# Summing the retrieved v rows in 64x64 quarters of the PE array, in a one-core encoder layer

## Chip, core and metric

The kernel runs on one core of one Trainium2 chip. The metric is the device time of one execution in microseconds (us). Before the change it is 2211.79 us, the median of three runs (2210.6 to 2211.9).

## The reference

One encoder layer for 512 tokens of width 1024 in float32: a gated mixer of a state-space layer and latent attention, a cross-attention over 256 memory tokens, and a retrieval of single-neuron experts; then a final norm. The change lies in the retrieval. Per token and head (8 heads), 16 experts are picked out of 16,384 by two lists of 128 keys; each has a row u and a row v of 1024 floats.

```python
s1, i1 = lax.top_k(s[:, :, 0], PEER_TOPK)
s2, i2 = lax.top_k(s[:, :, 1], PEER_TOPK)
cand_s = (s1[..., :, None] + s2[..., None, :]).reshape(T, PEER_HEADS, PEER_TOPK * PEER_TOPK)
cand_i = (i1[..., :, None] * PEER_N_KEYS + i2[..., None, :]).reshape(...)
top_s, pos = lax.top_k(cand_s, PEER_TOPK)
idx = jnp.take_along_axis(cand_i, pos, axis=-1)
gate = jax.nn.softmax(top_s, axis=-1)
u = jnp.take(u_emb, idx, axis=0)
act = jax.nn.gelu(jnp.einsum('thkd,td->thk', u, xc).astype(jnp.float32))
vv = jnp.take(v_emb, idx, axis=0)
return jnp.einsum('thk,thkd->td', (gate * act).astype(vv.dtype), vv)
```

## The kernel before

The kernel is written engine by engine, each with its own instruction list and explicit semaphores. The mixers and the cross-attention fill roughly the first 800 us; the retrieval fills the rest.

The retrieval works on groups: group g = 4h + t is head h (0 to 7) and token tile t (0 to 3, 128 tokens on the 128 partitions). A group has 16 slots, one expert per token and slot. For each slot POOL issues one indirect DMA that gathers 128 rows of 4 KB, partition p getting the row of token p, from `peer_u` into a ring of 8 places (`Ub`) and from `peer_v` into one of 16 places (`Vb`).

Who does what in period g:

- POOL (`head`, L1873) issues u of slot s of group g+1 and v of slot s of group g in turn. It waits for `dots` before it reuses a place of `Ub` (L1865) and for `v_summed` before it reuses one of `Vb` (L1870). All gathers are recorded under L1860.
- DVE (`head`, L1384): in the third tile of a head it copies the next head's scores (L1332); it picks the 16 best for group g+2 (`topk`, L1336 to L1356); it adds the finished sum of group g-1 to the residual H (`take_sum`, L1376); it forms the 16 dot products of group g+1 as the u rows land (L1367); then the 16 weights of group g+1 (`weights`, L1371) and the gates of group g+2 (L1358). Each small instruction is waited for before the next.
- ACT (`head`, L885) copies queries, takes the exponentials of the gates of g+2, and turns each of the 16 weights of group g into a diagonal matrix of 128x128 (L882; a ring of 8, `DRING`), then the gelu of g+1 (L875).
- PE (`head`, L1735) forms the next head's queries (L1710) and scores (L1720) ahead of the first two tiles, and then the weighted sum as matmuls: diagonal times v rows, 2 halves of 512 columns for each slot, accumulated over the 16 slots in two of the banks 0 to 3 (L1731). Even and odd tiles use different pairs of banks, so PE waits only for the sum of group g-2.
- SP loads the next head's 1 MB of query weights once PE has used the last ones, and at the end stores the output.

After the last group DVE takes its sum and normalises the rows (L1401 to L1410).

Of the kernel before, what the change touches and what calls it, by code (L numbers as in the profile page):

```python
# [29 lines left out]
U32 = mybir.dt.uint32  # L30
ALU = mybir.AluOpType
# [3 lines left out]
P = 128  # L35
# [154 lines left out]
def encoder_layer(nc, x, mem, positions, g_mix, w_in, b_gate, ssm_lam_re, ssm_lam_im, ssm_log_dt,  # L190
# [4 lines left out]
    with ctx:  # L195
# [3 lines left out]
        def sem(name):  # L199
            return ctx.enter_context(nc.semaphore(name))  # L200
# [25 lines left out]
        def reg(lo, *shape, base=R, parts=P):  # L226
            n = int(np.prod(shape))
            v = base[0:parts, lo:lo + n]
            names = "abcd"[:len(shape)]
            if len(shape) > 1:  # L230
                v = v.rearrange(f"p ({' '.join(names)}) -> p {' '.join(names)}",
                                **dict(zip(names, shape)))
            return v
# [62 lines left out]
        qhs = [reg(0, T), reg(512, T)]  # L296
        SC = reg(1024, NT, 2, NK)
        Vb = [reg(3072 + D * i, D) for i in range(VRING)]
        diag = [reg(19456 + P * i, P) for i in range(DRING)]
        gprow = reg(23040, D)  # L300
        gfrow = reg(24064, D)
        prod = reg(25088, D)
# [55 lines left out]
            sem(n) for n in ("qw_in", "q_filled", "q_copied", "s_filled", "s_copied")]  # L358

        idx_ready, gates_neg, gates_exp = [sem(n) for n in ("idx_ready", "gates_neg", "gates_exp")]  # L360
        dots, gelu_done, w_ready, diag_done, v_summed = [
            sem(n) for n in ("dots", "gelu_done", "w_ready", "diag_done", "v_summed")]
        acc_taken, final_done = sem("acc_taken"), sem("final_done")
# [222 lines left out]
        def _(act):  # L586
# [274 lines left out]
            def queries_out(h, s, first=False):  # L861

                act.wait_ge(q_filled, h * 2 + (s + 1))
                if not first:
                    act.wait_ge(s_filled, h * 2 + (s - 1))
                cols = slice(P if first else 0, T)
                act.activation(qhs[s][:, cols], ps[4 + s][:, cols], ACT.Copy).then_inc(q_copied, 1)

            def gate_exponentials(g):
                act.wait_ge(gates_neg, g + 1)  # L870
                act.activation(ex, cv, ACT.Exp, bias=nmx, accum_out=esum).then_inc(gates_exp, 1)
# [5 lines left out]
            def diagonals(g, t, first=False, slots=range(TOPK)):  # L877
                act.wait_ge(w_ready, g + 1)
                for s in slots:
                    if not first or s >= DRING:  # L880
                        act.wait_ge(v_summed, g * TOPK + (s - DRING + 1))
                    act.activation(diag[s % DRING], ident, ACT.Copy,  # L882
                                   scale=wgt[t % 2][:, s:s + 1]).then_inc(diag_done, 1)

            def head(h, first=False, last=False):  # L885
# [17 lines left out]
            def final_root(t):  # L903
                act.wait_ge(var_done, len(PARTS) + t + 1)
                act.activation(stat[:, 72 + t:73 + t], stat[:, 68 + t:69 + t], ACT.Sqrt).then_inc(std_done, 1)

            queries_out(0, 0, True)
            queries_out(0, 1, True)
            gate_exponentials(0)
            gate_exponentials(1)  # L910
            gelu_of(0)
# [9 lines left out]
        def _(dve):  # L921
# [391 lines left out]
            def lstep(ins):  # L1313

                count[0] += 1
                ins.then_inc(c_loop, 1)
                dve.wait_ge(c_loop, count[0])
# [18 lines left out]
            def topk(t):  # L1336

                for s in range(2):
                    top16(SC[:, t, s, :], sc1, tv[:, s, :], ti[:, s, :])
                lstep(dve.tensor_copy(tif, ti))  # L1340
                lstep(dve.tensor_tensor(cand.rearrange("p (a b) -> p a b", a=TOPK),
                                        tv[:, 0, :].unsqueeze(2).to_broadcast([P, TOPK, TOPK]),
                                        tv[:, 1, :].unsqueeze(1).to_broadcast([P, TOPK, TOPK]), ALU.add))
                top16(cand, cand1, cv, cpos)
                lstep(dve.tensor_scalar(nmx, cv[:, 0:1], -1.0, None, ALU.mult))
                dve.sem_inc(gates_neg, 1)
                lstep(dve.tensor_scalar(cpp[:, 0:16], cpos, 4, None, ALU.logical_shift_right))
                lstep(dve.tensor_scalar(cpp[:, 16:32], cpos, 15, None, ALU.bitwise_and))
                lstep(dve.tensor_copy(cpf, cpp))
                lstep(dve.tensor_tensor(eq, iota16.unsqueeze(1).to_broadcast([P, 2 * TOPK, TOPK]),  # L1350
                                        cpf.unsqueeze(2).to_broadcast([P, 2 * TOPK, TOPK]), ALU.is_equal))
                e4 = eq.rearrange("p (s k) a -> p s k a", s=2)
                lstep(dve.tensor_tensor(e4, e4, tif.unsqueeze(2).to_broadcast([P, 2, TOPK, TOPK]), ALU.mult))
                lstep(dve.tensor_reduce(isel, eq, AX.X, ALU.add))
                lstep(dve.scalar_tensor_tensor(idx[t], isel[:, 0:16], float(NK), isel[:, 16:32], ALU.mult, ALU.add))
                dve.sem_inc(idx_ready, 1)  # L1356

            def gates_of(g, t):  # L1358
# [11 lines left out]

            def weights(g, t):  # L1371
                dve.wait_ge(gelu_done, g + 1)
                lstep(dve.tensor_tensor(wgt[t % 2], gel, gate[t % 2], ALU.mult))
                dve.sem_inc(w_ready, 1)

            def take_sum(g, t):  # L1376

                dve.wait_ge(v_summed, (g + 1) * TOPK)
                for n in range(2):
                    h = H[:, t, 512 * n:512 * n + 512]  # L1380
                    lstep(dve.tensor_tensor(h, ps[2 * (t % 2) + n][:, :], h, ALU.add))
                dve.sem_inc(acc_taken, 1)

            def head(h, first=False, last=False):  # L1384
# [56 lines left out]
        def _(pe):  # L1441
# [279 lines left out]
                ins.then_inc(s_filled, 1)  # L1721


            def group(g, t, taken=True):
                if taken:
                    pe.wait_ge(acc_taken, g - 1)
                for s in range(TOPK):
                    pe.wait_ge(ld_v[s], (g + 1) * 16)
                    pe.wait_ge(diag_done, g * TOPK + (s + 1))
                    for n in range(2):  # L1730
                        last = pe.matmul(ps[2 * (t % 2) + n][:, :], diag[s % DRING], Vb[s][:, 512 * n:512 * n + 512],  # L1731
                                         start=(s == 0), stop=(s == TOPK - 1))
                    last.then_inc(v_summed, 1)

            def head(h, first=False, last=False):  # L1735
                for t in range(NT):
                    if t < 2 and not last:
                        queries(h + 1, t)
                        scores(h + 1, t)
                    group(h * NT + t, t, taken=not first or t >= 2)  # L1740

            for b in range(8):
                pe.wait_ge(drained[b], uses[b])
# [11 lines left out]
        def _(pool):  # L1755
# [103 lines left out]
            def gather(dst, table, ix, s, signal):  # L1859
                pool.indirect_dma_start(out=dst, out_offset=None, in_=table,  # L1860
                                        in_offset=bass.IndirectOffsetOnAxis(ap=ix[:, s:s + 1], axis=0)).then_inc(signal, 16)
# [6 lines left out]
            def v_row(g, t, s, first=False):  # L1868
                if not first:
                    pool.wait_ge(v_summed, g * TOPK + (s - (VRING - 1)))  # L1870
                gather(Vb[s], peer_v, idx[t], s, ld_v[s])

            def head(h, first=False, last=False):  # L1873
                for t in range(NT):
# [49 lines left out]
```

## Time and profile before

| | |
|---|---|
| median of three runs | 2211.79 us |
| the profiled execution | 2210.13 us, of which the span of its instructions 2208.3 us |
| busy in the span | PE 1804.8 us (82%), DVE 1450.7 (66%), POOL 1168.7 (53%), ACT 557.3 (25%) |
| L1731, matmul of diagonals and v rows | 2048 records, 973.8 us busy |
| L1860, gathers | 1024, 537 MB of the 603 MB that DMA moves |
| L882, diagonals | 512, 180.5 us busy, 394 ns each |
| chain that ended last | PE 37%, POOL 25%, DVE 16%, issue 11%, DMA 8%, ACT 3% |

How to read it: busy times say how much an engine worked, not that it set the pace. A timeline row has the start, the duration, the engine, the line, the instruction with its operands, the count, and in brackets the idle time before it with what ended it; "issue" is idle time in which nothing visible was awaited. One matmul of float32 shows as two records. "Landing" is the end of a DMA, seen here as the start of the instruction that waited for it.

### The profile page before, as it was taken

The numbers are of one execution on the slowest core, as the hardware profiler recorded it, in microseconds if no ns is written. First come the engines' busy times: TensorE is split into PE (matmuls) and PEld (weight loads), VectorE is DVE, ScalarE is ACT, GpSimd is POOL, SyncE is SP. The second block draws the span as 40 slices with busy tenths as digits, with TensorE's granted clock in tenths as the row PEclk, the third lists the DMA queues.
The fourth block names the chain that finished last, engine by engine and source line by source line (L and its number), as shares of the span: only waits on it lengthen the run. The fifth ranks groups of instructions, "written<-read, shape, count | busy, mean of one in ns | idle before, by whom it ended". The sixth has DMA issues, their size and how long they took to land.

```text
span 2208.3 us, 19211 instructions
## 1 busy us (share of the span) xinstructions
PE 1804.8 (82%) x5927; PEld 979.4 (44%) x5927; DVE 1450.7 (66%) x2986; ACT 557.3 (25%) x1159; POOL 1168.7 (53%) x1175
## 2 busy tenths in 40 slices
PE   6787798999998973969868878977877877887687
PEld 6455534787996761423323323323323322333233
DVE  5497675434444447777677677767767776776763
ACT  2323444222433121222112212212211221221211
POOL 6990000000001016777777777777777777777774
PEclk9889699999999995989989999999999999999899
DMA  4311401334342028999999999999999999999997
GB/s 117 61 16 20 105 1 34 86 100 140 95 133 68 20 82 346 395 393 408 401 397 408 406 393 410 403 392 408 376 398 401 406 390 403 410 400 398 409 399 295
DMA packets 239391, 603.06 MB, mean 273 GB/s; under 512 B 38533, under 2 KB 105274, under 8 KB 239290
## 3 DMA queue, kind: packets, MB, share of 16 engines
q0 software_dynamic: 147840, 537.99, 62.0%
q1 hardware_dynamic: 91450, 63.85, 10.5%
q8 instruction: 49, 0.80, 0.2%
q14 instruction: 52, 0.43, 0.1%
HBM read 597.56 MB, written 2.10 MB: 272 GB/s over the span
## 4 chain that ended last, share of the span: by engine, by line
PE 37%; POOL 25%; DVE 16%; issue 11%; DMA 8%; ACT 3%; SPq 0%; DVEq 0%; ACTq 0%; POOLq 0%
PE bank L1458 20%; PE bank L1731 15%; POOL R L1860 11%; POOL WS L1860 6%; POOL slabs L1860 5%; DMA WS<-in_peer_u,R 4%; DMA R<-in_peer_v,R 3%; DVE R L931 3%; PE bank L1710 2%; DVE R L1367 1%; PE bank L1447 1%; POOL R L1764 1%; POOL WS L1764 1%; DVE R L1199 1%; DVE stat L1192 1%
## 5 line engine op out<-in xcount | busy, mean ns | idle before, releaser
L1731 PE MATMUL bank<-R 128*128 128x512 f32 x2048 | 973.8, 624 | 243.1 <-ACT R L882 143.2
L1731 PEld LDWEIGHTS bank<-R 128*128 128x128 f32 x2048 | 387.8, 198 | 820.3 <-issue 570.6
L1860 POOL DMA_INDIRECT R<-in_peer_v,R x512 | 502.0, 980 | 156.0 <-issue 139.5
L1367 DVE CUSTOM_DVE_ANT_0 R<-WS,XN 128x1024 f32<-128x1024 f32 x256 | 313.6, 1225 | 176.4 <-DMA WS<-in_peer_u,R 171.8
L1367 DVE CUSTOM_DVE_ANT_0 R<-slabs,XN 128x1024 f32<-128x1024 f32 x256 | 313.7, 1226 | 125.7 <-DMA slabs<-in_peer_u,R 115.0
L1860 POOL DMA_INDIRECT slabs<-in_peer_u,R x256 | 259.4, 1013 | 209.0 <-DVEq L1356 96.2
L1860 POOL DMA_INDIRECT WS<-in_peer_u,R x256 | 262.1, 1024 | 78.0 <-issue 78.0
L1856 POOL TENSOR_TENSOR FTr<-slabs,FTr 128x2048 fp32r<-128x2048 f32 x1 | 4.5, 4494 | 536.3 <-ACT FTr L624 536.3
L882 ACT ACTIVATE R<-cst,R 128x128 f32<-128x128 f32 x512 | 180.5, 394 | 345.4 <-PE bank L1731 343.6
L1458 PE MATMUL bank<-R 128*128 128x64 f32 (+5 forms) x596 | 190.7, 463 | 45.9 <-ACT R L680 19.8
L1458 PEld LDWEIGHTS bank<-R 128*128 128x128 f32 (+3 forms) x596 | 89.8, 183 | 118.9 <-issue 75.5
L875 ACT ACTIVATE R<-R 128x16 f32<-128x16 f32 x32 | 6.9, 216 | 479.1 <-DVE R L1367 479.1
L964 DVE TENSOR_TENSOR WSr<-slabs,WSr 128x1024 fp32r<-128x1024 f32 (+2 forms) x47 | 60.7, 1292 | 99.8 <-ACT WSr L624 99.8
L1710 PE MATMUL bank<-FT,slabs 128*128 128x512 f32 (+1 forms) x256 | 112.0, 592 | 14.2 <-DMA slabs<-in_w_peer_q 11.6
L931 DVE TENSOR_TENSOR R<-R 128x512 f32<-128x512 f32 (+4 forms) x95 | 74.1, 780 | 32.6 <-POOLq L1844 26.5
L1458 PE MATMUL bank<-Rr,WSr 128*128 128x512 f32 (+1 forms) x448 | 95.4, 366 | 0.0
L1458 PEld LDWEIGHTS bank<-Rr,WSr 128*128 128x128 f32 x448 | 77.7, 189 | 13.7
L1710 PEld LDWEIGHTS bank<-FT,slabs 128*128 128x128 f32 x256 | 49.6, 194 | 73.5 <-issue 57.7
L1447 PE MATMUL bank<-cst,R 128*128 128x128 f32 (+2 forms) x300 | 48.0, 297 | 25.8 <-DVE R L1199 21.9
L624 ACT ACTIVATE WSr<-slabs 128x1024 fp32r<-128x1024 f32 (+2 forms) x48 | 53.9, 1125 | 59.2 <-PE bank L1458 59.2
L1458 PE MATMUL bank<-XNr,WSr 128*128 128x512 f32 x256 | 61.8, 393 | 1.9 <-DVE WSr L964 1.9
L1458 PE MATMUL bank<-FTr,WSr 128*128 128x512 f32 x256 | 63.2, 389 | 0.1
(210 smaller groups left out, 1903.4 us busy)
## 6 DMA issues: line engine op xcount, KB each, us to landing
slabs<-in_w_in SPq DMA_DIRECT2D x17, 512.0 KB, 5.3
slabs<-in_w_mem_kv SPq DMA_DIRECT2D x8, 1024.0 KB, 5.6
slabs<-in_w_peer_q SPq DMA_DIRECT2D x8, 1024.0 KB, 16.3
R<-in_peer_v,R POOLq DMA_INDIRECT x512, 6.6
slabs<-in_w_in SPq DMA_DIRECT2D x4, 1024.0 KB, 13.1
slabs<-in_w_ssm_glu SPq DMA_DIRECT2D x16, 256.0 KB, 3.2
slabs<-in_w_out SPq DMA_DIRECT2D x4, 1024.0 KB, 5.1
slabs<-in_w_mem_q SPq DMA_DIRECT2D x4, 1024.0 KB, 5.2
```

The costliest lines, as they stand in the source:

```text
L624: act.activation(hi, src, ACT.Copy).then_inc(w_hi, 1)
L882: act.activation(diag[s % DRING], ident, ACT.Copy, scale=wgt[t % 2][:, s:s + 1]).then_inc(diag_done, 1)
L931: step(dve.tensor_tensor(out, a, b, op))
L964: dve.tensor_tensor(lo, src, hi, ALU.subtract).then_inc(w_lo, 1)
L1192: step(dve.tensor_reduce(c, b[:, 0:width], AX.X, ALU.max))
L1367: dve.tensor_tensor_reduce(prod, Ub[s % URING], xn[:, t, :], 1.0, 0.0, ALU.mult, ALU.add, act_row[:, s:s + 1]).then_inc(dots, 1)
L1447: last = pe.transpose(dst, src, ident[0:n, 0:n])
L1458: last = pe.matmul(dst, lhs, rhs, start=(n == 0), stop=(n == len(terms) - 1))
L1710: ins = pe.matmul(ps[4 + s][:, cols], qw[:, k, columns(s)], FT[:, k, cols], start=(k == 0), stop=(k == KD - 1))
L1731: last = pe.matmul(ps[2 * (t % 2) + n][:, :], diag[s % DRING], Vb[s][:, 512 * n:512 * n + 512], start=(s == 0), stop=(s == TOPK - 1))
L1764: step(pool.tensor_tensor(out, a, b, op))
L1860: pool.indirect_dma_start(out=dst, out_offset=None, in_=table, in_offset=bass.IndirectOffsetOnAxis(ap=ix[:, s:s + 1], axis=0)).then_inc(si ...
```

## The change

The 64 partitions of each half of the array work by themselves. A diagonal of 128x128 has only two non-zero blocks of 64x64; both are now stored in 64 columns (partition p has its weight in column p mod 64, made from the constant `fold`). An even slot is summed by the quarters (0,0) and (64,64). For an odd slot the v rows are gathered turned by 64 tokens, so that partition p holds the row of token (p + 64) mod 128; its weights are turned in the same way, and it is summed by the quarters (0,64) and (64,0). Quarters that read partitions 0 to 63 write banks 0 and 1, those that read 64 to 127 write banks 2 and 3, so each token tile's sum is the sum of two banks for each 512 columns. For this

- `topk` writes a second list of indices `idxv` for the odd slots, turned, in two instructions of 64 partitions;
- `weights` is three instructions instead of one, for even slots, and for the two halves of the odd ones;
- `take_sum` adds four banks instead of two;
- PE handles slots in pairs: 8 matmuls of 64x64 by 512 columns for two slots, and it waits for the sum of group g-1 instead of g-2, since every group uses all four banks;
- ACT builds diagonals of 128x64, and the constant `fold` once at the start.

The number, size and order of the gathers stay as they are.

```diff
-        diag = [reg(19456 + P * i, P) for i in range(DRING)]
+        diag = [reg(19456 + 64 * i, 64) for i in range(DRING)]
+        fold = reg(19456 + 64 * DRING, 64)
+        idxv = [reg(20032 + 8 * i, 8).bitcast(U32) for i in range(NT)]
...
-                    act.activation(diag[s % DRING], ident, ACT.Copy,
+                    act.activation(diag[s % DRING], fold, ACT.Copy,
                                    scale=wgt[t % 2][:, s:s + 1]).then_inc(diag_done, 1)
...
+            for lo in (0, 64):
+                act.activation(fold[lo:lo + 64, :], ident[lo:lo + 64, lo:lo + 64], ACT.Copy).then_inc(fold_set, 1)
...
                 lstep(dve.scalar_tensor_tensor(idx[t], isel[:, 0:16], float(NK), isel[:, 16:32], ALU.mult, ALU.add))
+
+                for lo in (0, 64):
+                    there, here = slice(lo, lo + 64), slice(64 - lo, 128 - lo)
+                    lstep(dve.scalar_tensor_tensor(idxv[t][there, :], isel[here, 1:16:2], float(NK),
+                                                   isel[here, 17:32:2], ALU.mult, ALU.add))
...
-                lstep(dve.tensor_tensor(wgt[t % 2], gel, gate[t % 2], ALU.mult))
+                w, c = wgt[t % 2], gate[t % 2]
+                lstep(dve.tensor_tensor(w[:, 0:16:2], gel[:, 0:16:2], c[:, 0:16:2], ALU.mult))
+                for lo in (0, 64):
+                    there, here = slice(lo, lo + 64), slice(64 - lo, 128 - lo)
+                    lstep(dve.tensor_tensor(w[there, 1:16:2], gel[here, 1:16:2], c[here, 1:16:2], ALU.mult))
...
-                for n in range(2):
-                    h = H[:, t, 512 * n:512 * n + 512]
-                    lstep(dve.tensor_tensor(h, ps[2 * (t % 2) + n][:, :], h, ALU.add))
+                for half in range(2):
+                    for n in range(2):
+                        h = H[:, t, 512 * n:512 * n + 512]
+                        lstep(dve.tensor_tensor(h, ps[2 * half + n][:, :], h, ALU.add))
...
-            def group(g, t, taken=True):
-                if taken:
-                    pe.wait_ge(acc_taken, g - 1)
-                for s in range(TOPK):
+            def group(g, t):
+                if g:
+                    pe.wait_ge(acc_taken, g)
+                for s in range(0, TOPK, 2):
                     pe.wait_ge(ld_v[s], (g + 1) * 16)
-                    pe.wait_ge(diag_done, g * TOPK + (s + 1))
+                    pe.wait_ge(ld_v[s + 1], (g + 1) * 16)
+                    pe.wait_ge(diag_done, g * TOPK + s + 2)
                     for n in range(2):
-                        last = pe.matmul(ps[2 * (t % 2) + n][:, :], diag[s % DRING], Vb[s][:, 512 * n:512 * n + 512],
-                                         start=(s == 0), stop=(s == TOPK - 1))
-                    last.then_inc(v_summed, 1)
+                        for odd in range(2):
+                            for lo in (0, 64):
+                                to = 64 - lo if odd else lo
+                                ins = pe.matmul(ps[2 * (lo // 64) + n][to:to + 64, :],
+                                                diag[(s + odd) % DRING][lo:lo + 64, :],
+                                                Vb[s + odd][lo:lo + 64, 512 * n:512 * n + 512],
+                                                start=(s == 0), stop=(s == TOPK - 2))
+                            if n:
+                                ins.then_inc(v_summed, 1)
...
-                gather(Vb[s], peer_v, idx[t], s, ld_v[s])
+                if s % 2:
+                    gather(Vb[s], peer_v, idxv[t], s // 2, ld_v[s])
+                else:
+                    gather(Vb[s], peer_v, idx[t], s, ld_v[s])
```

## Rows read from the trace of the kernel before

**Rows 1.** The page, the span in 40 slices: granted clock, share of DMA, rate.
```profile
PEclk9889699999999995989989999999999999999899
DMA  4311401334342028999999999999999999999997
GB/s 117 61 16 20 105 1 34 86 100 140 95 133 68 20 82 346 395 393 408 401 397 408 406 393 410 403 392 408 376 398 401 406 390 403 410 400 398 409 399 295
```

**Rows 2.** Waits of POOL, 845 to 2200 us: engine, line, releaser: us, times, longest.
```profile
POOL slabs L1860 <- DVE R L1367: 38.8, 12, 10.5
...
POOL R L1860 <- PE bank L1731: 16.4, 54, 0.3
```

**Rows 3.** Timeline, group 4 to group 5: start us, us, engine, line, instruction.
```profile
995.64 1.23 DVE L1367 CUSTOM_DVE_ANT_0 R<-slabs,XN 128x1024 f32<-128x1024 f32 x1 [0.19 <-DVE H L1381]
...
997.99 0.96 POOL L1860 DMA_INDIRECT slabs<-in_peer_u,R  x1 [0.30 <-issue]
...
1016.26 1.02 POOL L1860 DMA_INDIRECT WS<-in_peer_u,R  x1 [0.30 <-issue]
...
1022.89 1.23 DVE L1367 CUSTOM_DVE_ANT_0 R<-WS,XN 128x1024 f32<-128x1024 f32 x1 [1.31 <-DMA WS<-in_peer_u,R]
...
1037.26 1.23 DVE L1367 CUSTOM_DVE_ANT_0 R<-slabs,XN 128x1024 f32<-128x1024 f32 x1 [0.19 <-DVE H L1381]
```

**Rows 4.** Timeline of group 7, which follows a group with copies of scores.
```profile
1124.23 1.23 DVE L1367 CUSTOM_DVE_ANT_0 R<-slabs,XN 128x1024 f32<-128x1024 f32 x1 [0.19 <-DVE H L1381]
...
1125.73 1.80 POOL L1860 DMA_INDIRECT slabs<-in_peer_u,R  x1 [4.09 <-DVE R L1367]
...
1144.21 1.00 POOL L1860 DMA_INDIRECT WS<-in_peer_u,R  x1 [0.30 <-issue]
...
1150.83 1.23 DVE L1367 CUSTOM_DVE_ANT_0 R<-WS,XN 128x1024 f32<-128x1024 f32 x1 [1.32 <-DMA WS<-in_peer_u,R]
```

**Rows 5.** Timeline of DVE: steps between two groups of dot products.
```profile
1110.77 1.42 DVE L1332 COPY R<-bank 128x512 f32<-128x512 f32 x2
...
2086.09 0.18 DVE L1373 TENSOR_TENSOR R<-R 128x16 f32<-128x16 f32 x1 [0.35 <-ACT R L875]
...
2094.10 0.17 DVE L1347 TENSOR_SCALAR R<-R 128x16 uint32<-128x16 uint32 x1
2094.31 0.21 DVE L1348 TENSOR_SCALAR R<-R 128x16 uint32<-128x16 uint32 x1
...
2096.95 0.17 DVE L1355 SCALAR_TENSOR_TENSOR R<-R 128x16 uint32<-128x16 f32 x1
2097.27 1.42 DVE L1381 TENSOR_TENSOR H<-bank,H 128x512 f32<-128x512 f32 x2
```

**Rows 6.** Timeline: first dot products of groups 2 and 30; a late landing.
```profile
910.75 1.23 DVE L1367 CUSTOM_DVE_ANT_0 R<-slabs,XN 128x1024 f32<-128x1024 f32 x1 [0.19 <-DVE H L1381]
...
1268.52 1.01 POOL L1860 DMA_INDIRECT WS<-in_peer_u,R  x1 [0.30 <-issue]
...
1277.73 1.23 DVE L1367 CUSTOM_DVE_ANT_0 R<-WS,XN 128x1024 f32<-128x1024 f32 x1 [1.33 <-DMA WS<-in_peer_u,R]
...
2098.87 1.23 DVE L1367 CUSTOM_DVE_ANT_0 R<-slabs,XN 128x1024 f32<-128x1024 f32 x1 [0.19 <-DVE H L1381]
```

**Rows 7.** Timeline of the tail: PE, DVE, POOL, and one window of all engines.
```profile
2166.89 1.98 PE L1731 MATMUL bank<-R 128*128 128x512 f32 x4 [0.70 <-DMA R<-in_peer_v,R]
2169.93 29.45 PE L1731 MATMUL bank<-R 128*128 128x512 f32 x68 [1.06 <-DMA R<-in_peer_v,R]
...
2171.96 1.42 DVE L1381 TENSOR_TENSOR H<-bank,H 128x512 f32<-128x512 f32 x2 [1.98 <-PE bank L1731]
...
2185.28 0.94 POOL L1860 DMA_INDIRECT R<-in_peer_v,R  x1 [0.30 <-issue]
...
2199.42 1.42 DVE L1381 TENSOR_TENSOR H<-bank,H 128x512 f32<-128x512 f32 x2 [19.00 <-PE bank L1731]
...
2192.00:2193.00 1.00, 1.00 (x4) 0.50 (x3) 0.00 (x0) 0.00 (x0) 0.00 (x0) 1.00 0.30 119
```

More of the change, by code:

```diff
@@ L360, in encoder_layer @@
         idx_ready, gates_neg, gates_exp = [sem(n) for n in ("idx_ready", "gates_neg", "gates_exp")]
+        fold_set = sem("fold_set")
         dots, gelu_done, w_ready, diag_done, v_summed = [
@@ L905, in final_root @@
                 act.activation(stat[:, 72 + t:73 + t], stat[:, 68 + t:69 + t], ACT.Sqrt).then_inc(std_done, 1)
+            for lo in (0, 64):
+                act.activation(fold[lo:lo + 64, :], ident[lo:lo + 64, lo:lo + 64], ACT.Copy).then_inc(fold_set, 1)
             queries_out(0, 0, True)
             queries_out(0, 1, True)
+            act.wait_ge(fold_set, 2)
             gate_exponentials(0)
@@ L1739, in head @@
                         scores(h + 1, t)
-                    group(h * NT + t, t, taken=not first or t >= 2)
+                    group(h * NT + t, t)
             for b in range(8):
```

## The prediction

> **What bounds the kernel now.** I read the page first. In the last 24 of the 40 slices the DMA share stands at 9 and the rate near 400 GB/s [rows 1]; before them there is nothing that the change touches but a little set-up. The stretch is the retrieval: 32 groups (8 heads by 4 token tiles), each gathering 16 rows of u and 16 rows of v for 128 tokens, 1,024 gathers of 512 KB in all. Next I read the waits of POOL, which issues every gather. It waits for DVE's dot products, 38.8 us in 12 waits, and hardly for PE: 54 times, 0.30 us at most [rows 2]. That 0.30 us is the step that stands between any two gathers, waited or not [rows 3]. So PE, though it is the busiest engine, holds nothing in the middle of the stretch; halving its work there is worth nothing by itself.
>
> What I then looked for is the loop that comes next. The ring for u has 8 places, so POOL may issue the gather into slot 8 of a group only when the group's first dot product is done. In an undisturbed group [rows 3]: the first dot product starts at 995.64; the gather of slot 8 starts 2.35 us later; that of slot 15 18.27 us after it; its dot product starts 6.63 us after that; and 14.37 us later, at 1037.26, the next group's first one starts. The loop is 41.62 us. POOL had 0.85 us to spare at slot 8: where it really is held, slot 8 starts 1.50 us after the first dot product instead of 2.35 [rows 4]. In group 7, after a group with two copies of scores (1.42 us, [rows 5]), the spare is gone and POOL stands idle 4.09 us; its next instruction takes 1.80 us where 0.96 is usual [rows 3, 4]. From slot 8 to slot 15 it is then 18.48 us, and the landing takes 6.62 us as before.
>
> The reader should see from this that POOL's own pace and the round trip through DVE are nearly equal, and that anything put between the last dot product of one group and the first of the next lengthens the second. Over the 28 periods from group 2 to group 30 the mean is (2098.87 - 910.75) / 28 = 42.43 us [rows 6].
>
> **The change on DVE.** Three things are added there, each exactly between two groups of dot products. (a) The sum is taken from four banks instead of two: two more adds of 128x512 out of a bank. The two of before take 1.42 us [rows 5], so +1.42, and 0.04 for the steps: +1.46. (b) Two more instructions write the turned indices. Line 1355, the like of them with 16 columns, takes 0.17 us, and small instructions of this chain start 0.21 apart [rows 5]: +0.42. (c) The weights take three instructions instead of one (0.18 us, [rows 5]): again two steps, +0.42. Together +2.3 us for each gap. That the 64-partition forms move data to other partitions is shown by no row. I bound their cost by zero below and by a 0.7 us add above, the 128x512 form; I take the small neighbours, which have nearly the same size.
>
> What this makes of a period: 1.50 (slot 8 after the first dot product, POOL now held) + 18.48 + 6.62 + 14.37 + 2.26 = 43.23 us, against 41.62: +1.61 us [rows 3, 4]. The 0.85 us that POOL had to spare covers part of the gap, and the slower restart (1.80 us) is within the 18.48. From below: if the queue ahead of a landing is shortened by the new stalls, the landings that are late now come earlier. One such landing took 9.21 us, 1268.52 to 1277.73 [rows 6], 2.6 us more than usual, and there are seven heads at most with one; 28 x 1.61 less 7 x 1.8 is 33 us. From above: all of the gap in every period, 28 x 2.26 = 63 us. I take 28 x 1.61 = **45 us**. The step from group 1 to group 2 is held by DVE already and takes the whole 2.3; the indices of group 0 and the gap after it add 1.2 more: **+3.5 us**. From group 30 to 31 no candidates are picked, DVE comes early, and I cost it at nothing.
>
> **The change on PE.** A pair of slots was 2 x 4 records of matmul, 0.433 us apart (29.45 us for 68, [rows 7]): 3.46 us. Now it is 16 records of the same 512 columns. One after another they take 6.93 us a pair; two at a time 3.46; four at a time 1.73. No row shows quarters side by side, so these are the bounds. Each product is two records, that is two passes over the same quarter, and the second pass of one stands in the queue before the first of the next. If records start in order, only the second pass of one quarter and the first of the next can run together. I therefore take two at a time: PE gains nothing.
> The Trainium skill (TensorE: Matmul & The Clock Gate, Part 3) says the same of order, that matmuls begin and end strictly as issued, and gives 3.07x for four packed row tiles. The skill's TensorEngine Tiling (Array Packing), Theoretical Speedup, allows up to 2x for each halved dimension, 4x here. By the first rule the end is as I take it, by the second it is the "four at a time" case; no row before shows either.
>
> There is one new wait: all groups share the four banks, so PE starts group g only when the sum of group g-1 is taken, just before the first dot product of a period. Behind that wait stand 27.7 us (16 slots x 1.73) of matmuls, and for two groups in four 16 more records of queries, about 7 us; they must end before the next sum is taken, 41 us later. They do. POOL asks for the first v place of the next group some 23 us after PE's start and then every 2.5 us; PE frees one each 1.7 us. ACT's diagonals run 8 slots ahead, as before, and get narrower; its work on gates and gelu is queued behind them and is wanted only at the period's end. The row of granted clocks has slices of 8 in this stretch, so PE runs at times at 1.2 instead of 2.4 GHz [rows 1]; at that level throughout, a group would take 27.7 us with four together, which fits, and 55 with two, which does not. While data comes in at 2.5 us a slot PE has 5 us for a pair, so I count on no more than short spells of it, as now. The sizes of the gathers do not change.
>
> **The tail.** Before, PE ran 68 records from 2169.93 to 2199.38 and DVE took the sum at 2199.42 [rows 7]. Now the last group waits for the sum of group 30: from 2171.96, 2 x 1.42 us and a step, to 2174.9. With two at a time, 16 x 1.73 = 27.7 gives 2202.6, that is +3.2; the last sum has two more adds, +1.4: **+4.6 us**. With four at a time PE would wait for data: the last gather is issued at 2185.28, the DMA share falls to 0.30 in 2192 to 2193 [rows 7], and one pair more ends at 2194: -5.4 + 1.4 = -4.0.
>
> **Sum.** 45 + 3.5 + 4.6 = 53 us. The profiled execution took 2210.13 us, its span 2208.3, and the median of the runs is 2211.79; differences carry over unchanged: 2211.8 + 53 = **2265 us**. With its own bounds this case reaches from 2211.8 + 33 + 3.5 - 4.0 = 2244 to 2211.8 + 63 + 3.5 + 4.6 = 2283.
>
> **Rivals.** (1) *Absorbed* (12%). The queue of the DMA engines, which are at full share even in undisturbed groups [rows 1], is what keeps a landing at 6.6 us. Stalls of 2 us then eat only that queue, and the mean period stays 42.4. For it: the full share. Against it: in group 7 a stall of 4 us left the landing of slot 15 at 6.62 [rows 4]. It gives 2211.8 + 3.5 and the tail's -4.0 or +4.6: 2211 to 2220. (2) *Freed* (6%). v places, and so PE, do hold POOL in a way that the waits don't show; then a group falls towards POOL's own 32 x 1.24 us = 39.7 us, 28 x 2.7 = 76 us less: 2136. Against it: waits for PE of 0.30 us only [rows 2]. (3) *Not side by side* (7%), slower by another road, and the case in which the change does not do what it says. At 6.93 us a pair a group costs 55.4 us, plus 2.9 for the sum that PE now awaits and about 2 for queries: 60 against 42.4, so some 30 x 18 = 540 us, and 32 in the tail: about 2780. It decides from 41 us of matmuls a group on, that is 5.1 us a pair. (4) The forecast (75%).
>
> **Chances.** A difference of 0.2%, 4.4 us, is about what can be told from no change. Faster: rival 2 and a part of rival 1, 0.08. Within 0.2%: most of rival 1's lower half, 0.05. Slower: 0.87. The range that holds 8 in 10 takes in the forecast's bounds and the space towards rival 1, in which some of the stalls are absorbed: 2224 to 2284.
>
> **What the changed profile would show.** The gap from the last dot product of a group to the next first one longer by 2.3 us; about 30 waits of POOL for DVE's dot products instead of 12, and their sum near 75 us instead of 39; periods near 43.2 us, 46 to 47 after the copies of scores; DMA share dipping once a period and the rate some 3% lower; PE starting each group just after the sum; 16 records a pair in 3.5 us. PE's waits for DVE show in place of those for ACT. I would be wrong if POOL showed waits for PE of several us (rival 3), if landings after a stall fell well below 6.6 us and stayed there (rival 1), or if the small 64-partition instructions cost much more than 0.2 us.

## The result, and the profile after

The changed kernel takes 2266.31 us (median of four runs, 2262.27 to 2269.95), the kernel before 2211.85 in the same comparison: a ratio of 1.0239, 95% interval 1.0212 to 1.0266. It is slower by 54.5 us; forecast were 53. The profiled execution took 2267.39 us, its span is 2265.6 us, 57.3 more than the span before; what is read from traces below is of one execution each.

The page of the changed kernel, its 40 slices and three groups of instructions (busy us, mean ns, idle before):

```profile
PEclk9888799999999977677768867878777767776687
DMA  4301401334421068999999999999999999999997
GB/s 114 66 10 19 103 0 51 89 89 150 129 94 56 20 229 321 378 376 392 402 364 382 406 376 368 407 375 383 399 372 392 384 373 395 383 367 374 387 376 302
...
L1751 PE MATMUL bank<-R 64*64 64x512 f32 x4096 | 676.2, 807 | 591.6 <-issue 315.7
...
L885 ACT ACTIVATE R<-R 128x64 f32<-128x64 f32 x512 | 139.3, 336 | 346.9 <-PE bank L1751 345.4
...
L1397 DVE TENSOR_TENSOR H<-bank,H 128x512 f32<-128x512 f32 x128 | 88.5, 691 | 26.6 <-PE bank L1751 18.7
```

Against [rows 1] the rate has lost some 4% in the second half (over 1000 to 2000 us 385 instead of 401 GB/s), and the granted clock of PE is 6 to 8 where it was 9: PE now works in short bursts, its matmuls of the weighted sum are 676 us busy instead of 974, and most bursts run wholly or in part at the lower of its two levels. The diagonals take 336 instead of 394 ns. None of these savings shows in the time.

The waits of POOL, 845 to 2260 us, and the same view as [rows 2]:

```profile
POOL slabs L1883 <- DVE R L1378: 96.5, 31, 11.2
...
POOL R L1883 <- PE bank L1751: 22.9, 75, 0.3
```

POOL waits for the dot products 31 times instead of 12, at slot 8 in each of groups 1 to 30 and once more, and 58 us longer in sum. For PE it still never waits more than 0.3 us. One period, group 16 to 17, by the timeline (as [rows 3]):

```profile
1534.43 1.23 DVE L1378 CUSTOM_DVE_ANT_0 R<-slabs,XN 128x1024 f32<-128x1024 f32 x1 [0.19 <-DVE H L1397]
...
1535.93 1.80 POOL L1883 DMA_INDIRECT slabs<-in_peer_u,R  x1 [2.22 <-DVE R L1378]
...
1554.43 1.00 POOL L1883 DMA_INDIRECT WS<-in_peer_u,R  x1 [0.30 <-issue]
...
1561.08 1.22 DVE L1378 CUSTOM_DVE_ANT_0 R<-WS,XN 128x1024 f32<-128x1024 f32 x1 [1.33 <-DMA WS<-in_peer_u,R]
...
1562.67 0.17 DVE L1385 TENSOR_TENSOR R<-R 128x8 f32<-128x8 f32 x1 [0.35 <-ACT R L878]
1562.87 0.36 DVE L1388 TENSOR_TENSOR R<-R 64x8 f32<-64x8 f32 x2
...
1574.03 0.17 DVE L1361 SCALAR_TENSOR_TENSOR R<-R 128x16 uint32<-128x16 f32 x1
1574.23 0.36 DVE L1365 SCALAR_TENSOR_TENSOR R<-R 64x8 uint32<-64x8 f32 x2
...
1574.74 2.87 DVE L1397 TENSOR_TENSOR H<-bank,H 128x512 f32<-128x512 f32 x4
1577.79 1.23 DVE L1378 CUSTOM_DVE_ANT_0 R<-slabs,XN 128x1024 f32<-128x1024 f32 x1 [0.19 <-DVE H L1397]
```

1.50 + 18.50 + 6.65 + 16.71 = 43.36 us; the forecast built 43.23. The reader should see the three additions: two weight instructions of 64 partitions in 0.36 us, two index instructions in 0.36, and the sum, whose four adds take 2.87 us instead of 1.42 for two. Over all 28 periods (first dot products of groups 2 and 30):

```profile
913.60 1.23 DVE L1378 CUSTOM_DVE_ANT_0 R<-slabs,XN 128x1024 f32<-128x1024 f32 x1 [0.19 <-DVE H L1397]
...
2156.68 1.23 DVE L1378 CUSTOM_DVE_ANT_0 R<-slabs,XN 128x1024 f32<-128x1024 f32 x1 [0.19 <-DVE H L1397]
```

(2156.68 - 913.60) / 28 = 44.40 us against 42.43 [rows 6]: 1.96 us more, 55.0 in all. By parts, means over these groups:

| us | before | after |
|---|---|---|
| first dot product to gather of slot 8 | 2.09 | 1.50 |
| slot 8 to slot 15 | 18.43 | 18.81 |
| slot 15 to its dot product (landing) | 7.14 | 6.95 |
| last dot product to the next first | 14.77 | 17.13 |
| period | 42.43 | 44.40 |

The rest of the 57.3 us of span: groups 1 to 2 +2.6, start of the retrieval +0.3, from group 30 to the last gather +0.4, and from the last gather to the end -0.9 us.

The tail:

```profile
2243.52 0.93 POOL L1883 DMA_INDIRECT R<-in_peer_v,R  x1 [0.30 <-issue]
...
2253.21 1.95 PE L1751 MATMUL bank<-R 64*64 64x512 f32 x16 [0.54 <-issue]
...
2255.24 2.87 DVE L1397 TENSOR_TENSOR H<-bank,H 128x512 f32<-128x512 f32 x4 [15.32 <-PE bank L1751]
```

PE's last pair is done 11.6 us after the last gather was issued; before it was 14.1 [rows 7]. The last gather itself lands 9.6 us after its issue, and 9.05 us in the kernel before, so PE now waits for data to the end.

### The profile page after: what moved, and what is told of

Its sections match the earlier page's. It is cut to its first block, busy times and chain, and to the rows that moved or that the text cites. A ratio compares the mean times of both kernels' runs of the same rounds, so it can differ in the third digit from the quotient of the medians.

```text
span 2265.6 us, 23277 instructions
## 1 busy us (share of the span) xinstructions
PE 1502.3 (66%) x7975; PEld 772.7 (34%) x7975; DVE 1518.8 (67%) x3178; ACT 516.2 (23%) x1161; POOL 1176.9 (52%) x1175
## 4 chain that ended last, share of the span: by engine, by line
PE 32%; DVE 29%; POOL 14%; issue 11%; DMA 11%; ACT 2%; SPq 1%; DVEq 0%; ACTq 0%; POOLq 0%
PE bank L1474 19%; PE bank L1751 11%; DMA WS<-in_peer_u,R 8%; POOL R L1883 6%; DVE H L1397 4%; POOL WS L1883 3%; DVE R L937 2%; DVE R L1378 2%; POOL slabs L1883 2%; DMA R<-in_peer_v,R 2%; DVE R L1328 2%; DVE R L1331 2%; DVE R L1329 2%; DVE R L1330 1%; DVE R L1327 1%
## 5 line engine op out<-in xcount | busy, mean ns | idle before, releaser
L1751 PE MATMUL bank<-R 64*64 64x512 f32 x4096 | 676.2, 807 | 591.6 <-issue 315.7
L1751 PEld LDWEIGHTS bank<-R 64*64 64x64 f32 x4096 | 188.5, 172 | 1065.1 <-issue 767.7
L1883 POOL DMA_INDIRECT slabs<-in_peer_u,R x256 | 275.0, 1074 | 261.3 <-DVE R L1378 96.5
L1883 POOL DMA_INDIRECT WS<-in_peer_u,R x256 | 256.4, 1001 | 78.1 <-issue 78.1
L885 ACT ACTIVATE R<-R 128x64 f32<-128x64 f32 x512 | 139.3, 336 | 346.9 <-PE bank L1751 345.4
L1397 DVE TENSOR_TENSOR H<-bank,H 128x512 f32<-128x512 f32 x128 | 88.5, 691 | 26.6 <-PE bank L1751 18.7
```

The lines of the kernel that those rows point to most:

```text
L885: act.activation(diag[s % DRING], fold, ACT.Copy, scale=wgt[t % 2][:, s:s + 1]).then_inc(diag_done, 1)
L1397: lstep(dve.tensor_tensor(h, ps[2 * half + n][:, :], h, ALU.add))
L1751: ins = pe.matmul(ps[2 * (lo // 64) + n][to:to + 64, :], diag[(s + odd) % DRING][lo:lo + 64, :], Vb[s + odd][lo:lo + 64, 512 * n:512 * n + ...
```

## Experiments

The theory: what costs the time is the longer gap on DVE between two groups of dot products, since POOL may not gather into slot 8 of the u ring until the next group's first dot product. The rivals: PE's new wait for the sum; the work of PE in quarters itself; and that the transport sets the pace and swallows stalls.

**DVE work alone (e1_dve_only).** The kernel before, with the same DVE instructions, their results into scratch.

```diff
+                    lstep(dve.scalar_tensor_tensor(dumi[there, :], isel[here, 1:16:2], float(NK), isel[here, 17:32:2], ...
+                    lstep(dve.tensor_tensor(dumw[there, :], gel[here, 1:16:2], gate[t % 2][here, 1:16:2], ALU.mult))
                     lstep(dve.tensor_tensor(h, ps[2 * (t % 2) + n][:, :], h, ALU.add))
+                    lstep(dve.tensor_tensor(prod[:, 512 * n:512 * n + 512], ps[2 * (t % 2) + n][:, :], h, ALU.add))
```

> The kernel before, with only the DVE work of the change added as idle work: two more adds of 128x512 out of the banks into scratch, two 64-partition index instructions and two 64-partition weight instructions into scratch. PE, ACT and the gathers are those of before. Theory (the longer stretch between two groups of dot products is the cost): the gap grows by 2.4 us, the mean period from 42.43 to about 44.4, POOL waits for dot products about 96 us in 31 waits, time 2264 to 2272 us (the tail keeps PE's slow end, one more add than before). Rival (the new wait of PE for the sum, or the PE work itself, costs it): within 5 us of 2212.

Measured 2266.24 us (2261.36 to 2267.32), ratio 1.0230 (1.0202 to 1.0257): the changed kernel's time to 0.1 us in the medians (its base in this comparison was 2214.15), with PE, ACT and gathers untouched. Gap 17.13 us, mean period 44.46. Waits of POOL in its trace, 845 to 2260 us:

```profile
POOL slabs L1869 <- DVE R L1372: 87.8, 31, 11.2
...
POOL R L1869 <- PE bank L1740: 15.2, 50, 0.3
```

**The rest alone (e2_pe_only).** The changed kernel with two banks summed instead of four, unturned indices and plain weights (its result leaves out these parts of the sum).

```diff
-                for half in range(2):
+                for half in range(1):
...
-                    gather(Vb[s], peer_v, idxv[t], s // 2, ld_v[s])
+                    gather(Vb[s], peer_v, idx[t], s, ld_v[s])
```

> The changed kernel without its DVE additions: two banks instead of four are added to the residual, odd slots use the unturned indices and weights (these parts of the result are left out). PE, ACT, the new wait and the pairs stay. Theory: the gap is 14.8 us as before, the mean period 42.4, and the tail is shorter by 2 to 5 us, so 2205 to 2212 us. Rival (wait or PE work costs it): near 2260.

Measured 2212.66 us (2209.74 to 2221.52), ratio 1.0003 (0.9986 to 1.0020), gap 14.76 us, POOL's waits those of before:

```profile
POOL slabs L1875 <- DVE R L1373: 38.9, 11, 10.5
```

Quarters, pairs and the new wait together change nothing in the time that can be told from zero; the interval leaves 3 to 4 us either way. With the first run this puts the loss on DVE's additions. In the profiled execution of this run, parts stand against each other: the mean period is 42.82 us, 0.39 more than before (11 us over 28 periods), while the stretch from group 30 to the end is 4.2 us shorter and the first group comes 4 us earlier. Whether the 0.39 us is PE's or scatter a single trace can't say.

**More of the same (e3_more_adds).** Two further adds into scratch.

```diff
                         lstep(dve.tensor_tensor(h, ps[2 * half + n][:, :], h, ALU.add))
+                        if half:
+                            lstep(dve.tensor_tensor(prod[:, 512 * n:512 * n + 512], ps[2 * half + n][:, :], h, ALU.add))
```

> The changed kernel with two further adds of 128x512 into scratch in each sum (+1.45 us in the gap). Theory: no spare is left on POOL, so nearly all of it shows in each of 30 periods: +42 to +46 us on 2266, so 2308 to 2313 us. Rival (DMA queue absorbs part of a stall): under +25 us.

Measured 2300.02 us (2297.72 to 2301.6): 34 us more than the change, 8 to 12 less than I expected, and above the 25 of the rival. The gap grew by 1.42 us, the mean period by 1.26 (45.65), 35 us over 28 periods. The landing fell from 6.95 to 6.68 us: one of the 28 takes over 7.5 us, where six did. So a tenth of the added gap is absorbed, and of the time a fifth is missing (34 us where 30 x 1.42 would be 43); the rest of that lies outside these periods, where the first group starts 3.8 us earlier and the end after group 30 is 1.8 us shorter. That the late landings come from loads of query weights, and that stalls shorten the queue ahead of them, is argued: in the kernel before, four landings of 9.2 to 9.5 us belong to gathers issued about 8 us after such a load had landed, but no run takes the loads away.

**Order of the quarters (e4_order).** Both halves of 512 columns of a quarter one after the other.

```diff
-                    for n in range(2):
-                        for odd in range(2):
-                            for lo in (0, 64):
-                                to = 64 - lo if odd else lo
+                    for odd in range(2):
+                        for lo in (0, 64):
+                            to = 64 - lo if odd else lo
+                            for n in range(2):
```

> The changed kernel with the quarters in another order: both halves of 512 columns of one quarter follow each other, so four records in a row use the same quarter. If PE takes records strictly in order, a pair of slots needs about 13 steps of 0.43 us, 5.6 us instead of 1.95, which is above the 5.1 us in which a pair's data comes in, and the kernel slows to 2330 to 2400 us. If each quarter has a queue of its own, a pair stays near 2 us and the time at 2266. By the theory that PE has room, any pair time below 5 us gives 2266 plus at most 5 in the tail.

Measured 2262.72 us (2260.76 to 2265.2). PE in its trace, pairs of slots while rows land:

```profile
1638.48 1.97 PE L1751 MATMUL bank<-R 64*64 64x512 f32 x16 [1.47 <-issue]
1644.64 3.71 PE L1751 MATMUL bank<-R 64*64 64x512 f32 x16 [4.19 <-issue]
```

The changed kernel, for comparison:

```profile
1650.72 1.95 PE L1751 MATMUL bank<-R 64*64 64x512 f32 x16 [1.56 <-issue]
...
1680.37 3.69 PE L1751 MATMUL bank<-R 64*64 64x512 f32 x16 [3.11 <-issue]
```

A pair takes 1.97 us at full clock and 3.71 at the lower one, against 1.95 and 3.69. In the trace of e4 the records of a pair start four together, the next four some 0.43 us later. So four records in a row for one quarter do not hold up the other three. Strict order, on which I had built "two at a time", is not what happens.

**The sum out of the gap, kernel before (e5_before_moved).** The two adds follow the dot products of slots 10 and 11.

```diff
-            def dot_products(g, t):
+            def dot_products(g, t, between=()):
...
                     dve.wait_ge(dots, g * TOPK + (s + 1))
+                    if s >= 10 and s - 10 < len(between):
+                        between[s - 10]()
```

> The kernel before, with the two adds that take a group's sum moved from the gap into the idle time between the dot products of slots 10 to 12, where DVE waits 1.3 us for each landing. Theory: the gap shrinks by 1.6 us to 13.2. In ordinary periods POOL has spare already, so they gain little; in the periods after a stall and after score copies 1.6 us each come back: 10 to 20 us in all, 2192 to 2204 us against 2212. Rival (DMA transport alone sets the pace and stalls are absorbed): 2212.

Measured 2195.62 us (2193.79 to 2199.5), ratio 0.9913 (0.9893 to 0.9934): the gap costs time in the kernel before too, and 19 us of it come back. Gap 13.20 us, mean period 42.12 (9 us over 28 periods; the profiled execution, 2199.5 us, was the slowest of the six), eight waits for dot products:

```profile
POOL slabs L1870 <- DVE R L1367: 26.4, 8, 10.5
```

**Further in that direction (e7_lists_moved).** Score copies and the first ten steps of the choice go among the dot products of slots 8 to 15 as well.

```diff
-                        topk((t + 2) % NT)
+                        picks((t + 2) % NT)
...
+                        if t == 1 and not last:
+                            between = between + score_copies(h + 1)
+                        if g + 3 < NG:
+                            between = between + lists((t + 3) % NT)
```

> As the last, with the two score copies and the first ten steps of the choice of candidates (for the group after) moved among the dot products of slots 8 to 15 too; the gap then is near 9.5 us. Theory: POOL never waits for a dot product after group 1, and a period is what POOL and the transport need, 41 to 41.6 us: 28 x 1 us less than before, 2180 to 2192 us, and a further cut of the gap would bring nothing. Rival (DVE's gap is still what counts): a gain in proportion to the cut, 28 x 5 us, near 2080.

Measured 2200.22 us (2197.21 to 2210.02), ratio 0.9934 (0.9911 to 0.9956): not below the last, and 8 us above the end of what I expected. The gap is 9.19 us and POOL practically stopped waiting for DVE, yet the mean period of its profiled execution is 42.35 (that one took 2210.02 us, the slowest of the six). Queues of its trace from 1000 to 2000 us (share of the 16 engines):

```profile
q0 software_dynamic: 108619, 395.52, 100.3%
q1 hardware_dynamic: 5200, 5.24, 1.5%
```

And waits of POOL in the same stretch:

```profile
POOL R L1894 <- issue: 100.3, 329, 0.3
POOL slabs L1894 <- issue: 57.6, 189, 0.3
POOL WS L1894 <- issue: 57.3, 188, 0.3
POOL R L1894 <- PE bank L1765: 14.9, 49, 0.3
```

Here is a floor that the gap does not set: its cut from 13.20 to 9.19 us brings no time. What sets it isn't shown. One reading is the transport: 32 gathers of 512 KB and a quarter of a 1 MB load are 17.04 MB a period, 42.5 us at 401 GB/s, with the engines' share full; but this rate comes from the same stretch, so the sum only says that period and bytes agree. The other is POOL's own pace: it never stands idle for more than 0.3 us, and its 755 gathers of 1.02 us in the mean with 0.30 between them fill the 1000 us; 32 of them are 42.4 us. Undisturbed gathers of 0.94 us would need 39.7, and whether the longer ones are held back by the transport no run separates. By either reading the 41 to 41.6 us a period that I expected were too few. Either way the rival of absorbed stalls holds only once the gap is short.

**The sum out of the gap, changed kernel (e6_after_moved).** The same edit, four adds behind slots 10 to 13.

> The changed kernel with its four adds moved among the dot products of slots 10 to 13. The gap falls from 17.1 to 14.1 us, slightly under that of before, so the theory expects 2200 to 2212 us: the whole loss undone by moving the adds. PE then starts each group some 20 us later in the period and must still free its places in time; at 2 to 3.7 us a pair it needs 16 to 30 us. Rival (the late start of PE holds up v gathers): waits of POOL for PE of over 0.3 us, and a time above 2225.

Measured 2364.79 us (2361.37 to 2368.58), ratio 1.0675: 98 us worse than the change, where I expected the loss undone. Waits in its trace, 845 to 2300 us (sum in us, count, longest):

```profile
ACT R L885 <- PE bank L1760: 898.6, 122, 29.9
...
DVE R L1387 <- ACT R L878: 205.4, 31, 8.0
...
POOL R L1892 <- PE bank L1760: 114.8, 67, 5.3
```

One period of its timeline, the last of the four adds and PE's group behind it:

```profile
1647.66 0.69 DVE L1398 TENSOR_TENSOR H<-bank,H 128x512 f32<-128x512 f32 x1
...
1648.47 16.45 PE L1760 MATMUL bank<-R 64*64 64x512 f32 x128 [21.96 <-DVEq L1400]
...
1660.31 0.17 DVE L1387 TENSOR_TENSOR R<-R 128x8 f32<-128x8 f32 x1 [6.71 <-ACT R L878]
```

PE starts its group when the fourth add is done, some 23 us into the period. POOL's next v gathers wait for it, 5.3 us at most; and ACT stands behind PE with diagonals 8 to 15, so the gelu that is queued behind them, and the weights that DVE makes from it, come up to 8.0 us late. The parts of the period say which of the two costs the time. The mean gap is 20.74 us, where 14.1 was expected and 17.13 stood in the changed kernel; the mean period is 47.94, 3.54 more than there and 99 us over 28 periods. Slot 8 to slot 15 grew by 0.23 us only, and the landing fell by 0.33. So the late gelu, which lies in the gap, carries the loss, and POOL's waits for PE hardly add to it. Both chains were in my list of what stands behind the new wait; with the sum at the head of the period they have 20 us of room, and here none. The 128 records in 16.45 us also show the quarters with all data at hand: 0.129 us a record against 0.433 of the full array [rows 7], 3.4 times as dense, though the mean granted clock in this group was 0.85 and in those rows 1.00. At 1.00 in both the ratio is 3.9, by this row of the e10 trace, 0.111 us a record:

```profile
1143.76 7.10 PE L1760 MATMUL bank<-R 64*64 64x512 f32 x64 [1.12 <-ACT R L885]
```

**Triple PE work (e9_pe_triple).** Each quarter product is made three times, so its sum is three times that of the reference.

```diff
-                                ins = pe.matmul(ps[2 * (lo // 64) + n][to:to + 64, :],
-                                                ...
-                                                start=(s == 0), stop=(s == TOPK - 2))
+                                for again in range(3):
+                                    ins = pe.matmul(ps[2 * (lo // 64) + n][to:to + 64, :],
+                                                    ...
+                                                    start=(s == 0 and again == 0), stop=(s == TOPK - 2 and again == 2))
```

> The changed kernel with every quarter product done three times (the sums are three times too large). A pair of slots takes about 5.9 us at full clock, above the 5.1 us in which its rows land, so a group needs 47 us and 3 more for the sum that PE awaits: by the working of the third rival, periods of 50 to 53 us, 2430 to 2540 us. If PE had another place to catch up, the time would stay below 2350.

One run: 3052.53 us, over 500 us above the range that I expected. PE in its trace:

```profile
1624.17 62.08 PE L1752 MATMUL bank<-R 64*64 64x512 f32 x384 [3.02 <-DVEq L1398]
1686.17 7.13 PE L1726 MATMUL bank<-FT,slabs 128*128 128x512 f32 x16
...
1696.28 60.40 PE L1752 MATMUL bank<-R 64*64 64x512 f32 x384 [1.12 <-ACT R L885]
```

PE is now the bound, as the third rival had it, but a pair takes 7.8 us (7.55 in the second row, at a granted clock of 1.00) and not 5.9: with six records in a row for one quarter they run less side by side, 0.157 us each against the 0.111 of e10. Why six in a row do this and the four of e4 don't isn't shown. Periods are 65 to 72 us, 68.0 in the mean: the group's 60.4 to 62.1, plus queries, scores and sum. The mechanism of that rival is right, its pair time is what the change does not have.

**Early adds (e10_after_early, e11_before_early, e12_e5_again, e13_e10_again).** The adds follow the dot products of slots 0 to 3 (changed kernel) or 0 and 1 (kernel before); the third run is the e5 kernel, the fourth repeats the first. Against e6 and e5:

```diff
-                    if s >= 10 and s - 10 < len(between):
-                        between[s - 10]()
+                    if s < len(between):
+                        between[s]()
```

> The changed kernel with its four adds placed one by one behind the dot products of slots 0 to 3, where the rows have landed already and POOL asks for one freed place only every 2.5 us. The gap is 14.1 us, as with the adds behind slots 10 to 13, but PE may start a group some 8 us into the period instead of 23. If the loss of that earlier form (2365 us) came from the late start of PE, with v gathers and the gelu queued behind it, the waits of POOL for PE go back to 0.3 us and the time to 2190 to 2205 us. If it came from adds among dot products as such, it stays above 2260.

> The kernel before with its two adds behind the dot products of slots 0 and 1. By the theory equal to the form with the adds behind slots 10 and 11, 2193 to 2200 us: what counts is that they are out of the gap, not where they go.

> The kernel before with its two adds behind the dot products of slots 10 and 11, beside the last two on the same chip: 2193 to 2200 us. Against the form of the changed kernel with early adds it tells what quarters on PE are worth once the gap is paid for: by the theory only the tail, -5 to +2 us, less what four adds instead of two cost.

> The changed kernel with its four adds behind the dot products of slots 0 to 3, once more, since in the last three runs the kernel before itself took 2486 us, with pauses of 1 to 2 us between small DVE instructions in every kernel. Where the kernel before takes near 2212: gap 14.1 us, waits of POOL for PE of 0.3 us, 2190 to 2205 us if only the adds in the gap cost the time; 2225 or more if the later start of PE costs it.

In these four runs the kernel before took 2486 us (first three) and 2496 us (last), against 2212 to 2215 in all others, so none answers its expectation in us. The ratios to it are 1.0286 (1.0218 to 1.0354), 0.9739 (0.9679 to 0.9799), 0.9853 (0.9800 to 0.9907) and 1.0215 (1.0153 to 1.0277). DVE in the e12 trace, in the gap:

```profile
1342.44 0.24 DVE L1340 CAST R<-R 128x32 f32<-128x32 uint32 x1 [1.75 <-remote]
1343.83 0.43 DVE L1341 TENSOR_TENSOR R<-R 128x256 f32<-128x256 f32 x1 [1.15 <-DVE R L1340]
1345.23 0.43 DVE L1321 MAX8 R<-R 128x8 f32<-128x256 f32 x1 [0.97 <-DVE R L1341]
```

Small steps that follow each other within 0.3 us elsewhere stand 1 to 1.8 us apart, in every one of the four kernels; the mean gaps are 22 us for e12 and 24 for e10. What makes the pauses I can't tell from the traces. Three things can be read all the same. Removing the adds from the gap pays in the kernel before wherever they go (e11, e12; e11's interval lies just below e12's, so early is not worse). For PE, POOL in e10 waits 5.0 us in 13 waits, 1.4 at most, and in e13 0.3 at most, not the 115 us of e6: the early sum gives PE its room back. The chain through the gelu, which carried the loss of e6, is mostly gone too: from 900 to 2100 us DVE waits for it 24.5 us in 5 waits (e10) and 70.2 in 7 (e13), against 175.9 in 25 (e6), but single waits reach 18 us, and what causes these isn't shown. And the changed kernel with early adds is still slower than the kernel before under these conditions; whether it would be at or below 2212 us where that takes 2212 stays open.

## Why the prediction was right, point by point

- **What bounds.** Right: PE can be relieved of some 300 us of busy time without a gain (e2), and the round trip through DVE is what the change lengthens (e1).
- **The gap.** Forecast +2.3 us, measured +2.36: the 64-partition instructions that move data to the other half cost like their small neighbours (0.36 us for two). The forecast's own sum of the period took in 2.26 of its 2.30, 1 us over 28 periods.
- **The period.** Forecast +1.61 us, measured +1.96, inside the bounds of 33 to 63 us for the 28 periods (55). The term was 10 us too small because group 4, which I took as typical, has more to spare than the mean: slot 8 came 2.35 us after the first dot product there, 2.09 in the mean, since groups that are held already pay the whole gap; and slot 8 to 15 grew by 0.38 us instead of 0.21. The landing, taken as unchanged, got 0.19 us shorter, which works the other way. POOL's waits for the dot products came to 96.5 us, where near 75 was forecast.
- **The first groups.** Forecast +3.5; measured 2.6 + 0.3 = 2.9.
- **Quarters side by side.** Wrong. I took two at a time, 3.46 us a pair; it is four, 1.95 us. The step that failed is the order of records: the row of before shows two records per product, but not that other quarters must wait for the second, and they don't (e4). Of the two readings of the Trainium skill, the table of TensorEngine Tiling (Array Packing), Theoretical Speedup, came nearer: with up to 4x allowed, 3.6 were measured in a pair by itself (16 x 0.433 = 6.93 us against 1.95) and 3.9 in 64 records in a row (e10). The order of starts in TensorE: Matmul & The Clock Gate, Part 3, of the Trainium skill did not cost what I made of it (e4).
- **The tail.** Hence +4.6 was wrong: the four-at-a-time value was -4.0, and -0.9 was measured; PE waits for data there as in that case, but the data come later than I read from the falling DMA share: I let the last pair end 8.7 us after the last gather's issue, and that gather lands 9.05 us after it in the kernel before and 9.6 in the changed one. PE saves 2.5 us, and the sum's two adds take 1.45 back. These 5.5 us too much and the 10 too little of the period offset each other in part. That is luck, and it makes the total closer than its parts.
- **The new wait.** Costed at nothing, and it costs nothing (e2), because the sum comes at the head of the period. It is not free as such: with PE's start 23 us into the period the kernel takes 98 us more, by way of the late gelu (e6).
- **Lower clock.** I counted on short spells; in the changed kernel it is common (0.76 of full in 1000 to 2000 us against 0.95). Of 126 pairs that stand by themselves between 900 and 2230 us, 41 run wholly at full clock (1.95 us), 30 wholly at the lower level (3.69 us) and 55 in part. With four quarters together even the slow ones stay under the 5.1 us of a pair.
- **Rivals.** *Absorbed* is wrong for the change but right in part: in e3 a tenth of the added gap did not show in the period, and at a short gap there is a floor (e7), set by the transport or by POOL's own pace. *Freed* and *not side by side* are out by e2 and by the pair time.

The best kernel of the study is the one before with its sum taken among the dot products, 2195.62 us, 0.9% faster than before and 3% than the change.

## What to carry to other kernels

Before an engine is relieved, look who waits for it; here the busiest engine was waited for 0.3 us at a time, while a stretch of small steps on an engine that is busy two thirds of the time closed a loop through a ring of eight buffers with 0.85 us to spare. When work must be added to an engine, put it where that engine waits for data anyway, and check what hangs on the result's time: moving the sum to the same place is worth -19 us in one kernel and +98 us in the other. A forecast from one typical period should be weighed with the periods that are already held.

## What I had not expected of the hardware

- Four 64x64 quarters, two of which share rows and two of which share columns, ran side by side in float32: 64 records in 7.10 us at a granted clock of 1.00 (e10), and 1.95 to 1.97 us a pair in either order. With six records in a row per quarter the density fell to 0.157 us a record at the same clock (e9).
- POOL's first gather after a wait took 1.80 us instead of 0.94 to 0.96, in every one of groups 1 to 30 of the changed kernel, after waits of 1.0 to 11.2 us; in e10 it took 0.93 to 0.94 in groups 2 to 29, after waits of up to 14.2 us.
- No run moved more than 401 to 404 GB/s over 1000 us with gathers of 4 KB rows (before and e7 401, e5 404), with the 16 engines at full share. Whether this is a ceiling of the transport or POOL's pace of issue is open (e7).
- In four runs the kernel before took 12 to 13% more than in the others and the kernel of e5 11% more, with pauses of 1 to 1.8 us between small DVE instructions (e12); the cause is open.
